# RWKV core of a three-block network: matmul issue order over the array's quadrants, and where three products stand

## The reference, cut to what matters

```python
def _rwkv7_step(S, inp):
    r, w, k, v, a, b = inp
    sa = jnp.einsum('bhvk,bhk->bhv', S, a)
    S = S * w[:, :, None, :] + sa[..., None] * b[:, :, None, :] + v[..., None] * k[:, :, None, :]
    y = jnp.einsum('bhvk,bhk->bhv', S, r)
    return S, y
...
    w_log = -jax.nn.softplus(-(w0 + jnp.tanh(xw @ w1) @ w2)) - 0.5     # decay
    a = jax.nn.sigmoid(a0 + (xa @ a1) @ a2)                            # rate
    seq = (r, decay, k, v, -kk, kk * a)                                # per head, 64 channels
```

## Time and profile before

| | us |
|---|---|
| median of 3 runs | 2372.4 (2369.59 to 2377.89) |
| the profiled execution, its own time | 2370.42 |
| its span | 2368.5 |
| TensorE busy | 2203.1 |
| VectorE busy | 1308.4 |
| ScalarE busy | 929.1 |
| mean granted TensorE clock | 0.968 |

### The profile page before, as it was taken

The page is one execution under the profiler, slowest core; times in us unless marked ns, Lnnn a source line. Parts: engine busy times, 40 slices in busy tenths (PEclk is TensorE's granted clock), DMA queues, the critical chain, the costliest instruction groups (busy, mean ns, idle before and its releaser), DMA issues.

```text
span 2368.5 us, 37383 instructions
## 1 busy us (share of the span) xinstructions
PE 2203.1 (93%) x14830; PEld 1717.5 (73%) x14830; DVE 1308.4 (55%) x1978; ACT 929.1 (39%) x1471; POOL 99.4 (4%) x114
## 2 busy tenths in 40 slices
PE   4989999986899999879998999999799999999997
PEld 2856666665688888646776888888467787888886
DVE  4565777674564545584654645545654544434444
ACT  4573343332442332345654533323334444322222
POOL 0001111110000000100001000001000001000001
PEclk8989999997999999989999999999899999999999
DMA  3300000003133332201111232333120232332321
GB/s 124 98 30 27 15 18 24 6 3 122 58 107 98 97 98 91 78 27 42 40 54 63 89 106 89 100 95 90 57 71 27 63 115 84 103 98 98 98 85 66
DMA packets 53030, 168.89 MB, mean 71 GB/s; under 512 B 6920, under 2 KB 11144, under 8 KB 52768
## 3 DMA queue, kind: packets, MB, share of 16 engines
q1 hardware_dynamic: 52896, 167.00, 22.2%
HBM read 164.88 MB, written 2.10 MB: 71 GB/s over the span
## 4 chain that ended last, share of the span: by engine, by line
PE 83%; DVE 12%; ACT 2%; issue 1%; DMA 0%; SPq 0%; DVEq 0%; ACTq 0%
PE bank L1719 61%; PE bank L2153 2%; PE bank L1797 2%; PE bank L2046 2%; PE bank L1745 2%; PE bank L1880 1%; DVE rstd L1028 1%; PE bank L2083 1%; PE bank L2065 1%; PE bank L1861 1%; PE bank L2163 1%; DVE rw_k_inv L1172 1%; PE bank L1906 1%; DVE tmp L1057 1%; DVE tmp L1074 1%
## 5 line engine op out<-in xcount | busy, mean ns | idle before, releaser
L1719 PE MATMUL bank<-a_hi,w_hi 128*128 128x512 f32 x1424 | 571.9, 402 | 37.5 <-DVE w_lo L1022 20.1
L1719 PE MATMUL bank<-a_hi,w_lo 128*128 128x512 f32 x1424 | 558.2, 392 | 0.0
L1719 PE MATMUL bank<-a_lo,w_hi 128*128 128x512 f32 x1424 | 557.6, 392 | 0.0
L1022 DVE TENSOR_TENSOR w_lo<-w_raw,w_hi 128x1024 fp32r<-128x1024 f32 (+3 forms) x322 | 369.9, 1150 | 240.9 <-ACT w_hi L574 235.2
L574 ACT ACTIVATE w_hi<-w_raw 128x1024 fp32r<-128x1024 f32 (+3 forms) x322 | 311.4, 969 | 185.7 <-PE bank L1719 180.5
L1719 PEld LDWEIGHTS bank<-a_hi,w_hi 128*128 128x128 f32 x1424 | 269.5, 189 | 111.7 <-issue 35.1
L1719 PEld LDWEIGHTS bank<-a_hi,w_lo 128*128 128x128 f32 x1424 | 270.1, 190 | 60.0 <-issue 6.1
L1719 PEld LDWEIGHTS bank<-a_lo,w_hi 128*128 128x128 f32 x1424 | 269.6, 189 | 56.9
L1719 PE MATMUL bank<-b_hi,w_hi 128*128 128x512 f32 x640 | 254.6, 398 | 20.3 <-DVE b_lo L1080 19.7
L1719 PE MATMUL bank<-b_hi,w_lo 128*128 128x512 f32 x640 | 251.0, 392 | 0.0
L1719 PE MATMUL bank<-b_lo,w_hi 128*128 128x512 f32 x640 | 250.9, 392 | 0.0
(11 more groups left out here) (312 smaller groups left out, 3027.7 us busy)
## 6 DMA issues: line engine op xcount, KB each, us to landing
w_raw<-in_f0gu SPq DMA_DIRECT2D x44, 512.0 KB, 3.5
w_raw<-in_f1gu SPq DMA_DIRECT2D x44, 512.0 KB, 3.5
w_raw<-in_f2gu SPq DMA_DIRECT2D x44, 512.0 KB, 3.5
w_raw<-in_f0dn SPq DMA_DIRECT2D x16, 512.0 KB, 3.5
w_raw<-in_f1dn SPq DMA_DIRECT2D x16, 512.0 KB, 3.5
w_raw<-in_f2dn SPq DMA_DIRECT2D x16, 512.0 KB, 3.5
w_raw<-in_in SPq DMA_DIRECT2D x10, 512.0 KB, 3.6
w_raw<-in_r SPq DMA_DIRECT2D x8, 512.0 KB, 6.3
```

Source lines behind the costliest of these rows:

```text
L1022: dve.tensor_tensor(w_lo[r][:, 0:n, :], raw[r][:, 0:n, :], w_hi[r][:, 0:n, :].bitcast(F32), ALU.subtract).then_inc(w_split[r], 1)
L1719: mm = pe.matmul(bank[r][:, :], w[r][:, k, :], a[:, k, :], start=(k == 0 and n == 0), stop=(k == kt - 1 and n == 2))
```

## The change

It has five parts, all in the RWKV core:

1. The sets (1,2) and (0,2), and the sets (1,3) and (0,3), are issued interleaved, so that heads 0 and 1 alternate. DVE masks in the order (1,2), (0,2), (1,3), (0,3).
2. At level 1 the growth stands ahead of the k-a products. It waits for the masked set `(p, 2)`, whose bank it overwrites; the k-a products still wait for all eight.
3. For tiles 1 to 7 the rate product goes to bank 1 and is issued right after the decay product, at level 1, in place of level 2; it doesn't wait for `knorm_ready` any more.
4. The transitions (L1914) loop over `c`, `h`, `p` in place of `h`, `c`, `p`, and wait for `agate_ready` first.
5. The state increments are issued as all `k_nat` by `v_nat` products and then all `b_nat` by `u_nat` products, each over `c`, `h`, `p`.

```diff
-SCORES = ((0, 0), (0, 1), (1, 0), (1, 1), (1, 2), (1, 3), (0, 3), (0, 2))
+SCORES = ((0, 0), (0, 1), (1, 0), (1, 1), (1, 2), (0, 2), (1, 3), (0, 3))
+SCORE_PAIRS = (((0, 0),), ((0, 1),), ((1, 0),), ((1, 1),), ((1, 2), (0, 2)), ((1, 3), (0, 3)))
+        def rate_bank(q):
+            return 1 if q else 7
...
             def rate_product(q):
-                pe.wait_ge(knorm_ready, q + 1)
-                pe.matmul(bank[7][:, :], lora2[64:P, 0, :], ...)
+                if q == 0:
+                    pe.wait_ge(knorm_ready, 1)
+                pe.matmul(bank[rate_bank(q)][:, :], lora2[64:P, 0, :], ...)
...
             def bonus_sums(q):
-                pe.wait_ge(agate_ready, q + 1)
+                if q == 0:
+                    pe.wait_ge(agate_ready, 1)
...
+                for pair in SCORE_PAIRS:
...
+                            for p, n in pair:
+                                left, right = operands[n]
+                                mm[p] = pe.matmul(bank[score_bank(p, n)][HP[h], cols(c, CHUNK)], left[HP[p], chunk],
+                                                  right[HP[p], chunk], start=True, stop=True)
+                    for p, n in pair:
+                        mm[p].then_inc(scored, 1)
...
+                    for p in range(2):
+                        b = 4 - 4 * p
+                        pe.wait_ge(prod_ready, ...)
+                        if lv == 1:
+                            pe.wait_ge(masked, j * 8 + (SCORES.index((p, 2)) + 1))
...  (growth, now ahead of)
                     if lv == 1:
                         pe.wait_ge(masked, j * 8 + 8)
...  (k-a products)
                     if ahead and lv == 1:
                         v_steps(q, range(V_EARLY, 5))
                         pe.wait_ge(x_ready2, j + 1)
                         key_norms(q)
                         decay_product(q)
+                        rate_product(q)
                     elif ahead and lv == 2:
                         v_steps(q, (5,))
-                        rate_product(q)
...
+                if ahead:
+                    pe.wait_ge(agate_ready, q + 1)
-                for h in range(2):
-                    for c in range(TT):
+                for c in range(TT):
+                    for h in range(2):
                         for p in range(2):
                             mm = pe.matmul(bank[1 - h][HP[p], cols(c, HEAD)], w_nat[...], b_nat[...], ...)
...
-                for h in range(2):
+                for left, right in ((k_nat, v_nat), (b_nat, u_nat)):
                     for c in range(TT):
-                        for p in range(2):
-                            dst = bank[6 + h][HP[p], cols(c, HEAD)]
-                            pe.matmul(dst, b_nat[...], u_nat[...], start=True, stop=False, ...)
-                            mm = pe.matmul(dst, k_nat[...], v_nat[...], start=False, stop=True, ...)
+                        for h in range(2):
+                            for p in range(2):
+                                mm = pe.matmul(bank[6 + h][HP[p], cols(c, HEAD)], left[...], right[...],
+                                               start=(c == 0 and left is k_nat), stop=left is b_nat, ...)
```

More of the change, by code:

```diff
@@ L711, in prep_sigmoids @@
                 act.wait_ge(lora_done, q * 3 + 2)
-                act.activation(a_gate[:, :], bank[7][:, :], ACT.Sigmoid, bias=tv("a0")).then_inc(agate_ready, 1)
+                act.activation(a_gate[:, :], bank[rate_bank(q)][:, :], ACT.Sigmoid, bias=tv("a0")).then_inc(agate_ready, 1)
             def prep_decay(q, first=False):
@@ L1825, in front @@
                 pe.wait_ge(rdec_ready, q + 1)
[L1826 to L1835, removed]
+                operands = ((b_dec, a_dec), (b_dec, r_dec), (k_dec, a_dec), (k_dec, r_dec))
+                for pair in SCORE_PAIRS:
+                    for p, n in pair:
+                        if (p, n) == (1, 0):
+                            if last is not None:
+                                variance_of(last)
+                            pe.wait_ge(natural, q * 4 + 4)
+                        if (p, n) == (0, 2):
+                            pe.wait_ge(masked, q * 8 + (SCORES.index((0, 1)) + 1))
+                        if last is not None and (p, n) == (0, 3):
+                            pe.wait_ge(ystd_ready, last + 1)
+                    mm = {}
                     for c in range(TT):
@@ L1838, in front @@
                             chunk = cols(2 * c + h, CHUNK)
-                            mm = pe.matmul(bank[score_bank(p, n)][HP[h], cols(c, CHUNK)], left[HP[p], chunk],
-                                           right[HP[p], chunk], start=True, stop=True)
-                    mm.then_inc(scored, 1)
+                            for p, n in pair:
+                                left, right = operands[n]
+                                mm[p] = pe.matmul(bank[score_bank(p, n)][HP[h], cols(c, CHUNK)], left[HP[p], chunk],
+                                                  right[HP[p], chunk], start=True, stop=True)
+                    for p, n in pair:
+                        mm[p].then_inc(scored, 1)
             def mean_of(j):
@@ L1863, in core @@
                         mm.then_inc(z_done, 1)
+                    for p in range(2):
+                        b = 4 - 4 * p
+                        pe.wait_ge(prod_ready, j * 2 * LEVELS + (2 * (lv - 1) + p + 1))
+                        if lv == 1:
+                            pe.wait_ge(masked, j * 8 + (SCORES.index((p, 2)) + 1))
+                        else:
+                            pe.wait_ge(invt_ready, j * 2 * LEVELS + (2 * (lv - 2) + p + 1))
+                        for c in range(TT):
+                            for h in range(2):
+                                mm = pe.matmul(half_blocks(bank[b + 2][HP[h], cols(c, HEAD)], lv, 1),
+                                               prod[p][HP[h], c, :], half_blocks(inv_t[p][HP[h], c, :], lv, 1),
+                                               start=True, stop=True)
+                        mm.then_inc(grown, 1)
                     if lv == 1:
@@ L1926, in core @@
                     pe.wait_ge(bonus_ready, q + 1)
-                for h in range(2):
+                for left, right in ((k_nat, v_nat), (b_nat, u_nat)):
                     for c in range(TT):
-                        for p in range(2):
-                            dst = bank[6 + h][HP[p], cols(c, HEAD)]
[L1931 to L1934, removed]
+                        for h in range(2):
+                            for p in range(2):
+                                mm = pe.matmul(bank[6 + h][HP[p], cols(c, HEAD)], left[HP[h], c, HP[p]],
+                                               right[HP[h], c, HP[p]], start=(c == 0 and left is k_nat),
+                                               stop=left is b_nat, skip_group_check=True)
                 mm.then_inc(gain_done, 1)
```

12 lines of the change are left out of this document (2 added, 10 removed).

## The result

The changed kernel takes 2356.11 us (median of 5, 2355.16 to 2359.04), the kernel before 2376.7 us beside it (median of 5, 2369.59 to 2378.87). The ratio, which is that of the means, is 0.9923, with a 95% interval of 0.9904 to 0.9942: 0.77% faster, 18.3 us of 2376.7 (the medians lie 20.6 us apart), where 22.7 us were forecast. The forecast time was 2350, its range 2343 to 2361. The profiled execution took 2356.11 us, its span 2354.2 us, 14.3 us less than the span before.

A forecast was written before the change was run, and what follows sets the result against it. The bound was a chain of waits alternating between PE and DVE. Seven tiles x 2.14 = 15.0 us, last tile 2.2 and clock 5.5 made 22.7 us off the 2372.4 median: 2350 us, range 2343 to 2361.

The forecast's parts named there:

- Paired scores: Interleaved score sets in each RWKV tile: worth 0, since DVE is behind with masks and seeds meanwhile.
- Growth first: At level 1 PE restarts after the sixth mask in place of the eighth: 0.67 us a tile, bounds 0 and 0.67.
- Transitions: Transitions (L1914) on all four quadrants may save 0.3 us, hidden behind the bonus on DVE: 0.
- Decay and rate: Rate product runs beside the decay product at level 1, in full overlap: 1.05 us, net 0.90 us a tile.
- over 0.2 as a sign of being wrong: Sign against the forecast: a new wait of level-3 z on `rw_inv` longer than 0.2 us.
- would only move along: At levels 3 and 4, ACT's sigmoids hang on the same z and move with it; nothing else comes late.
- Increments: State increments on four quadrants take 0.95 us less on PE; 0.57 us a tile counted, bounds 0 and 0.57.
- Strict order of starts: Rival: matmuls start strictly in program order; transitions and increments gain nothing, decay and rate half; 2363 us, chance 0.05.
- Last tile: In the last tile, growth first saves about 1.6 us and the increments 0.6 us: 2.2 us.
- The clock of the last tile: K-a products refill PE's idle gap, so the granted clock stays at 1.00, not 0.50, through the levels: 5.5 us.
- The fall that I had as a rival, in tile 6's loop without value steps: Rival: the clock falls at other moments, as in tile 6's chunk loop; 3 to 4 us each, 2353 to 2359, chance 0.10.

## Why the prediction was right

The time came out inside the range, and the mechanism of the middle tiles is the forecast one, at a smaller size: the parts undone one by one add up to 0.55 + 0.91 + 0.37 = 1.83 us a clean tile, which gained 1.80; the standstills take 0.13 back on average. The clock is another matter. Its gains and losses, 3 to 6 us each, cancelled in good part, so that 2356 lies this near the forecast is partly luck.

- **Paired scores, 0 forecast:** 0.04 us less with them undone, nothing. Right, and for its reason.
- **Growth first, 0.67 forecast:** 0.50 by undoing it (0.55 in clean tiles), 0.58 in the chain. The mechanism is right; the term ignored that the wait on the sixth mask is handed over in 0.14 us and not in 0.04.
- **Transitions, 0 forecast:** not undone by themselves; in the middle tiles nothing is left over for them to explain.
- **Decay and rate, 0.90 forecast:** 0.91 to 0.94. Full overlap at 512 columns, on two row halves. The new late thing is the one named: z of head 1 at level 3 waits for the inverse. It waits 0.30 us there (z takes 1.45 us in place of 1.15), where I had reckoned with 0.15 lost and had named over 0.2 as a sign of being wrong. Behind it ACT's table load enters the chain, which I had said would only move along. Of the 0.14 us between 1.57 and 1.43 at the bonus, 0.09 is the hand-over of the mask and 0.05 is left for this.
- **Increments, 0.57 forecast:** 0.26 by undoing them, 0.37 in clean tiles, where 3.06 became 2.70. This is the term that was mis-sized. The gain's start moved by about the 0.31 us worked out; but I let the first state product follow the gain's end by 0.03 us, and it follows by 0.25. The rows had it: before, the gain ended at 363.88 + 0.75 = 364.63 and the product started at 364.92, 0.29 later. With 0.25 in the sum the term is 364.92 - (364.32 + 0.25) = 0.35 us. In tiles 2, 3 and 6 standstills took more. No row of the kernel before showed one, and the kernel with the increments undone has none, so it takes the faster increments for PE to run ahead of the supply of its program.
- **Strict order of starts:** falls. 32 L1944 of `v_nat` take 0.69 us, (0.69 - 0.22) / 31 = 15 ns each (0.22 being the length of a single one), and decay and rate start 0.01 us apart, though two decay instructions precede the first of the rate. The rule of the Trainium skill (TensorE: Matmul & The Clock Gate, Part 3, the mechanism) that matmuls start in strict order disagrees with both, in these fp32 products of 64 rows.
- **Last tile, 2.2 us forecast with a fallen clock:** 42.72 to 40.5 us in the kernel with unpaired scores, 2.2. That this agrees is luck. That kernel had lost 1.24 us to a low clock around the turn (its first growth is added 11.06 us behind it, against 9.82). At like clocks growth first is worth 1.5 us (1.6 forecast), the increments 0.7 (0.6 forecast; first increment to first state product is 3.04 us with them undone and 2.31 without), and the transitions 0.3 (0 forecast; first transition to first increment is 2.05 us before and 1.75 in the kernel with unpaired scores, both at 0.50). Together 2.5 us.
- **The clock of the last tile, 5.5 us forecast:** the step that failed is that the refilled gap keeps the clock up. The clock stayed up in the changed kernel alone; with the same gap, 1.63 of 3 us busy and not the 1.92 I compared it with, the clock fell in the kernel with the increments undone. Where it stayed up, the stretch from the first growth to the first increment took 17.45 us in place of 22.33, 4.9 us less and not 5.5, since a level took 2.78 us and not the 2.6 reckoned with. The tile as a whole gained only 3.2 us by it (40.5 to 37.36), as the low clock around its turn cost 1.3 us more than in the kernel compared with, and it fell again at the tile's end. The fall that I had as a rival, in tile 6's loop without value steps, came in the same run: clock 0.58 from 490 to 496. That rival's 2353 to 2359 holds the measured time too.
- **The rest of the clock:** the stretch ahead of the first turn (3.1 us gained) and what is lost behind RWKV (6.2 us) are outside what the change touches.

Structure alone gives 11.0 us by the turns of tiles 0 to 6 and 2.5 us of the last, 13.5 us or 0.57% of 2376.7 (14.2 us, 0.60%, with seven tiles of 1.67). The measured 0.77% has 0.58% to 0.96% as its interval, so structure lies at its lower edge. With the 5.4 us by which the last tile really was shorter it is 16.4 us, 0.69%. So of the size forecast, 22.7 us, the tiles were some 4 us too large (15.0 against 11.0), and the 5.5 us of clock are a term that the new order does not earn by itself.

## What to carry to other kernels

Small matmuls gain from being spread over row and column halves only where PE is what the next engine waits for. Ask of each group who consumes it, and what stands ahead of the consumer on its own engine: `k_dec` ahead of the gain held back as much (0.36 us a clean tile) as the increments' order gave (0.37). Two products on half the rows each are the best of such pairs where they can be had at full width, since one of them is then free. A term for the clock belongs in the range, not in the forecast, until several kernels with the same gap agree: here two profiles of one kernel did, and eight others with the same order did not. Where a fast group stands still without a wait, look when the packets of the `instruction` queue land before blaming banks or operands.

## What was not expected of the hardware

- PE stands still for 0.1 to 1.6 us where it has no wait, mostly where two four-quadrant groups of 64 MATMUL instructions follow each other (15 ns per start), and goes on 1.24 to 1.64 us after a 16 KB packet of its program has landed. It was in no tile of the kernel before, and its place moves when 160 instructions are put ahead.
- A wait of PE on DVE took 0.04 us from the eighth mask and 0.14 us from the sixth; 0.25 us from the gain. Why they differ is open.
- The granted clock stayed at 1.00 through the last tile's levels in 2 of 10 profiles of kernels with nearly the same last tile, both times in the same kernel.
